# Own start distance for each slot of the two weight rings in a one-core attention and RG-LRU layer

## The reference

```
z = rms_norm(x) @ w_in                 # 2048 x 11328, split into q, kv, rope, gates, u, merge gates
y_mla = (softmax(q k^T, chunk mask) v * silu(gate)) @ w_o_mla      # 16 heads
y_lru = (scan of the RG-LRU over the 4-tap causal convolution of u * silu(gate)) @ w_o_lru
merged = sigmoid(m_mla) * y_mla + sigmoid(m_lru) * y_lru
x = x + merged @ w_out
x = x + (p @ w_ple) * sigmoid(rms_norm(x) @ w_ple_gate)
out = rms_norm(x)
```

## Time and profile before

| | us |
|---|---|
| median of three runs | 2129.43 (2128.58 to 2131.06) |
| span of the profiled execution | 2126.2 |
| TensorE matmul busy | 2070.6 (97%), 9070 matmuls |
| TensorE weight load busy | 1661.5 (78%) |
| GpSimd busy | 910.8 (43%) |
| ScalarE busy | 718.2 (34%) |
| VectorE busy | 665.4 (31%) |
| DMA | 247 MB, mean 116 GB/s |

### The profile page before, as it was taken

The page is one execution under the profiler, slowest core; times in us unless marked ns, Lnnn a source line. Parts: engine busy times, 40 slices in busy tenths (PEclk is TensorE's granted clock), DMA queues, the critical chain, the costliest instruction groups (busy, mean ns, idle before and its releaser), DMA issues.

```text
span 2126.2 us, 25597 instructions
## 1 busy us (share of the span) xinstructions
PE 2070.6 (97%) x9070; PEld 1661.5 (78%) x9070; DVE 665.4 (31%) x952; ACT 718.2 (34%) x1251; POOL 910.8 (43%) x683
## 2 busy tenths in 40 slices
PE   7999999999999999999998999999999999999997
PEld 5788888888887878778776777778888888888885
DVE  5100000000013728364676445591010151111344
ACT  6322223222223443524344444422222222233232
POOL 2444444444444544545361321144444444444442
PEclk9999999999999999999999999999999999999998
DMA  6533333333322323233352412343332343224222
GB/s 229 178 118 100 118 118 117 121 118 118 116 102 88 110 79 102 96 118 94 108 121 79 138 61 64 113 179 132 123 118 100 118 156 138 82 98 180 99 99 99
DMA packets 128684, 247.00 MB, mean 116 GB/s; under 512 B 15053, under 2 KB 40309, under 8 KB 120565
## 3 DMA queue, kind: packets, MB, share of 16 engines
q1 hardware_dynamic: 116688, 185.09, 26.6%
q10 hardware_dynamic: 11941, 61.17, 7.7%
HBM read 214.26 MB, written 29.36 MB: 115 GB/s over the span
## 4 chain that ended last, share of the span: by engine, by line
PE 51%; issue 27%; POOL 17%; DVE 3%; ACT 1%; POOLq 1%; ACTq 0%; DVEq 0%
PE ps L1214 49%; POOL wlo L351 17%; PE ps L1412 1%; DVE qrf L990 0%; DVE qrf L986 0%; POOLq L350 0%; DVE pjlo L1059 0%; PE ps L1474 0%; ACT pjhi L669 0%; DVE x L1203 0%; DVE stage L988 0%; ACTq L555 0%; POOLq L347 0%; DVE vlo L1026 0%; DVE latkv L974 0%
## 5 line engine op out<-in xcount | busy, mean ns | idle before, releaser
L351 POOL TENSOR_TENSOR wlo<-raw,whi 128x512 fp32r<-128x512 f32 x672 | 909.5, 1357 | 1189.5 <-ACT whi L367 1188.9
L367 ACT ACTIVATE whi<-raw 128x512 fp32r<-128x512 f32 x672 | 422.3, 632 | 1217.6 <-PE ps L1214 1165.9
L1214 PE MATMUL ps<-hhi,whi 128*128 128x512 f32 x1408 | 556.7, 395 | 2.9 <-POOL wlo L351 2.9
L1214 PE MATMUL ps<-hhi,wlo 128*128 128x512 f32 x1408 | 556.2, 395 | 0.0
L1214 PE MATMUL ps<-hlo,whi 128*128 128x512 f32 x1408 | 556.1, 395 | 0.0
L1214 PEld LDWEIGHTS ps<-hhi,whi 128*128 128x128 f32 x1408 | 263.9, 187 | 69.4 <-POOL wlo L351 5.1
L1214 PEld LDWEIGHTS ps<-hhi,wlo 128*128 128x128 f32 x1408 | 263.9, 187 | 64.7
L1214 PEld LDWEIGHTS ps<-hlo,whi 128*128 128x128 f32 x1408 | 263.9, 187 | 64.4
L875 DVE TENSOR_TENSOR stage<-ps,stage 128x512 f32<-128x512 f32 x16 | 11.0, 690 | 515.4 <-ACT stage L466 513.9
L1214 PE MATMUL ps<-lhi,whi 128*128 128x512 f32 x256 | 101.9, 398 | 2.5 <-DVE llo L795 2.5
L1214 PE MATMUL ps<-llo,whi 128*128 128x512 f32 x256 | 101.8, 398 | 0.0
(11 more groups left out here) (249 smaller groups left out, 2462.4 us busy)
## 6 DMA issues: line engine op xcount, KB each, us to landing
raw<-in_w_in SPq DMA_DIRECT2D x88, 1024.0 KB, 5.0
raw<-in_w_o_lru SPq DMA_DIRECT2D x16, 1024.0 KB, 5.0
raw<-in_w_o_mla SPq DMA_DIRECT2D x16, 1024.0 KB, 5.0
raw<-in_w_out SPq DMA_DIRECT2D x16, 1024.0 KB, 5.1
raw<-in_w_ple_gate SPq DMA_DIRECT2D x16, 1024.0 KB, 5.0
sig_scr<-stage ACTq DMA_DIRECT2D x8, 1024.0 KB, 7.0
raw<-in_w_kv_b SPq DMA_DIRECT2D x32, 256.0 KB, 4.2
stage<-sig_scr ACTq DMA_DIRECT2D x8, 1024.0 KB, 4.8
```

What stands on the lines that cost most here:

```text
L351: pool.tensor_tensor(wlo[:, k % RING], raw[:, k // RAWC, k % RAWC], whi[:, k % RING].bitcast(F32), ALU.subtract).then_inc(lo_ready, 1)
L367: act.activation(whi[:, c % RING], raw[:, c // RAWC % 2, c % RAWC], ACT.Copy).then_inc(hi_ready, 1)
L1214: return pe.matmul(o, l, r, start=start, stop=stop)
```

## The change

The two rings become views of one tensor `ring`. Slot n of `whi` begins at 2048 n bytes plus a pad of 0, 64, 128 or 256 bytes; slot n of `wlo` at 2048 (4 + n) bytes plus 528, 608, 704 or 896 bytes. Unused tensors (`line_pad`, `small_pad`, `l_pad`, `m_pad`, `x1_pad`) shift the other tiles. Nothing is computed in another way.

```
+        sb("line_pad", [P, 96])
         raw = sb("raw", [P, 2, RAWC, W])
-        whi = sb("whi", [P, RING, W], F32R)
-        wlo = sb("wlo", [P, RING, W], F32R)
+        ring = sb("ring", [P, 2 * RING * W + 352], F32R)
+        whi = [ring[:, n * W + pad:(n + 1) * W + pad] for n, pad in enumerate((0, 16, 32, 64))]
+        wlo = [ring[:, (RING + n) * W + pad:(RING + n + 1) * W + pad] for n, pad in enumerate((132, 152, 176, 224))]
...
+        sb("small_pad", [P, 24])
...
-        ohi, olo, lhi, llo, merged = lay(
+        ohi, olo, _, lhi, llo, _, merged = lay(
+            ("ohi", [P, KD, S], F32R), ("olo", [P, KD, S], F32R), ("l_pad", [P, 24], F32),
+            ("lhi", [P, KD, S], F32R), ("llo", [P, KD, S], F32R), ("m_pad", [P, 32], F32),
+            ("merged", [P, KD, S], F32))
-        x1, x1hi, mhi, mlo, x1lo = lay(
+        x1, _, x1hi, mhi, mlo, x1lo = lay(
+            ("x1", [P, TT, D], F32), ("x1_pad", [P, 56], F32), ("x1hi", [P, KD, S], F32R),
...
-                    h, l = whi[:, slot, m * P:(m + 1) * P], wlo[:, slot, m * P:(m + 1) * P]
+                    h, l = whi[slot][:, m * P:(m + 1) * P], wlo[slot][:, m * P:(m + 1) * P]
```

More of the change, by code:

```diff
@@ L183, in trunk_layer @@
             ("qrf", [P, HEADS // 2, S], F32), ("qr", [P, 4, S], F32R))
-        ohi, olo, lhi, llo, merged = lay(
-            ("ohi", [P, KD, S], F32R), ("olo", [P, KD, S], F32R),
-            ("lhi", [P, KD, S], F32R), ("llo", [P, KD, S], F32R), ("merged", [P, KD, S], F32))
-        x1, x1hi, mhi, mlo, x1lo = lay(
-            ("x1", [P, TT, D], F32), ("x1hi", [P, KD, S], F32R),
+        ohi, olo, _, lhi, llo, _, merged = lay(
[4 more added lines that the diff above has]
+            ("x1", [P, TT, D], F32), ("x1_pad", [P, 56], F32), ("x1hi", [P, KD, S], F32R),
             ("mhi", [P, KD, S], F32R), ("mlo", [P, KD, S], F32R), ("x1lo", [P, KD, S], F32R))
-        _, plep, gfin = lay(("ple_r1", [P, R1], F32), ("plep", [P, NG, TT, W], F32), ("gfin", [P, D], F32))
+        _, plep, gfin = lay(("ple_r1", [P, R1 + 64], F32), ("plep", [P, NG, TT, W], F32), ("gfin", [P, D], F32))
         ps = ctx.enter_context(nc.psum_tensor("ps", [P, 8, 512], F32))
@@ L350, in _ @@
                     pool.wait_ge(hi_ready, i * (2 * RAWC) + (k + 1))
-                    pool.tensor_tensor(wlo[:, k % RING], raw[:, k // RAWC, k % RAWC],
-                                       whi[:, k % RING].bitcast(F32), ALU.subtract).then_inc(lo_ready, 1)
+                    pool.tensor_tensor(wlo[k % RING], raw[:, k // RAWC, k % RAWC],
+                                       whi[k % RING].bitcast(F32), ALU.subtract).then_inc(lo_ready, 1)
         @block.scalar
@@ L366, in split @@
                     act.wait_ge(chunk_used, i * stride + (c - RING + 1))
-                act.activation(whi[:, c % RING], raw[:, c // RAWC % 2, c % RAWC], ACT.Copy).then_inc(hi_ready, 1)
+                act.activation(whi[c % RING], raw[:, c // RAWC % 2, c % RAWC], ACT.Copy).then_inc(hi_ready, 1)
             act.dma_start(vrow[0:N1, 0, :], vectors).then_inc(vec_landed, 16)
@@ L1230, in tokens @@
                     h, l = ahi[:, m * P:(m + 1) * P], alo[:, m * P:(m + 1) * P]
-                    mm(o, h, whi[:, slot], first, False)
-                    mm(o, h, wlo[:, slot], False, False)
-                    ins = mm(o, l, whi[:, slot], False, last)
+                    mm(o, h, whi[slot], first, False)
+                    mm(o, h, wlo[slot], False, False)
+                    ins = mm(o, l, whi[slot], False, last)
                 return ins
@@ L1495, in _ @@
                     h, l = x1hi[:, k, t * P:(t + 1) * P], x1lo[:, k, t * P:(t + 1) * P]
-                    mm(ps[:, t], h, whi[:, slot], False, False)
-                    mm(ps[:, t], h, wlo[:, slot], False, False)
-                    ins = mm(ps[:, t], l, whi[:, slot], False, k == KD - 1)
+                    mm(ps[:, t], h, whi[slot], False, False)
+                    mm(ps[:, t], h, wlo[slot], False, False)
+                    ins = mm(ps[:, t], l, whi[slot], False, k == KD - 1)
                 ins.then_inc(last_done, 1)
```

## The result

| | before | after |
|---|---|---|
| median, us | 2130.24 (2128.58 to 2132.03) | 2117.07 (2114.45 to 2117.96) |
| span of the profiled execution, us | 2126.2 | 2112.7 |

Ratio 0.9937, 95% interval 0.9923 to 0.9951: so 13 us less, a change of 0.6% that is clear of the noise. The forecast was 2103 us, a gain of 26 us. The direction was right, the size forecast was twice what was measured.

What follows compares the result with a forecast made beforehand. The prediction took TensorE's matmul rate as the bound. Its terms, -27 + 1 + 0 = -26 us on 2126.2, gave a span of 2100 us and, with 3.2 us for the median, 2103 us; range 2042 to 2159 us.

Steps and rivals of the forecast that it cites:

- What bounds the kernel, and the unit price: TensorE's matmul rate sets the end; 8064 ring matmuls lie in sequence, so 1 ns on each is 8.06 us.
- The distance matters, against the rule of two ports that never wait: Operand start distance changes matmul gaps, 233.3 against 227.1 ns; by the documented rule it cannot matter and the sum is 0.
- Step (a): The 8064 ring matmuls: mean gap falls from 233.3 to 230 ns under the new distances, -27 us.
- Its bounds: Limits for the ring matmuls: -161 us if all reach 213.3 ns, +134 us if every one takes 250 ns.
- Step (b): Where TensorE waits for other engines, a faster TensorE waits longer; in attention half the gain may be lost, 1 us.
- Step (c): GpSimd, ScalarE, VectorE and DMA at other starts: GpSimd's 1.28 us piece stays covered below 2.76 us; taken as 0.
- Step (d): Products without rings (krw2, gates, attention's scores and values) keep their distances: no change.
- Rival, far distances: Ring matmuls at 96 to 256 bytes could be mostly free of extra cycles: 220 ns, -107 us, 2022 us; chance 0.16.
- Rival, mixing costs: Mixed distances at slot and chunk changes are slower than one common distance: 236.0 ns mean, +22 us, 2151 us; chance 0.28.

Runs made afterwards that it cites:

- experiment 2: All-at-0 kernel with activation tiles moved so the common distance is the old 32 bytes at other places, krw2 also 32 from hhi: 2132.04 us, one run.
- experiment 8: Changed kernel with other pads, two probes, one run each: small distances, 2113.01 us; high slots at 0 with low slots at -32 to -192, 2122.35 us.
- experiments 5 and 6: Changed kernel with slot 0's pads for all slots, 2110.92 us; then one common distance of 16, 128 or 64 bytes: 2106.86, 2124.99, 2121.52 us.
- experiment 1: Changed kernel with all ring slots and activation tiles starting at 0 modulo 512 bytes, activation pads taken out: 2081.13 us, ratio 0.9777 to the kernel before.
- experiment 5: Changed kernel with slot 0's pads for all slots: high at 0, low at 16 bytes, activation tiles at 0; 2110.92 us, ratio 0.9924 to before.

## Why the direction of the prediction was right and its size wrong

- *What bounds the kernel, and the unit price.* Right: TensorE's gaps alone, 8.06 us for each ns. After the change -1.8 ns gave -14.4 by this and -13.5 in the span; with all at 0, -52 and -46. One reading was too broad: the clock was below its upper level not only at the edges, but for a short while in attention too (0.99 in the earlier trace rows).
- *The distance matters, against the rule of two ports that never wait.* Right, and now shown by the krw2 product alone (experiment 2). By the Trainium skill, page SBUF — State Buffer, section "Who interferes with whom", TensorE reads its two operands through independent ports and never waits on anyone. The trace does not agree with the plain reading of it, that the rate is the same at any distance: 227.1 against 233.5 ns. Whether the difference is a wait at a read port, no run shows.
- *Step (a), "I take 230 ns".* The direction was right and this is the term that was mis-sized: 231.5 ns, -14 us instead of -27. The value was taken between krw2's settled 227.1 and unsettled 231 ns, as if all eight distances were near 0. The runs show that only a slot whose two distances are near 0 modulo 256 comes to 226.7 and that the others stay between 231.0 and 234.0 ns. In the changed kernel that is one slot of four, in the features form, outside of the lhi half of C_Y. One slot at 80 ns less, two at 20 less and one at none make 120 / 48 = 2.5 ns a gap in the stages with `hhi`, and 1 ns in the later ones.
- *Its bounds.* -161 and +134 us were far too wide. No common distance came out slower than 32 in a measurable way, and none under 226.7 ns; the slowest single slot took 235.7 ns a gap (experiment 8). The 250 ns of the upper bound is one of eight handovers in the trace before: from the full starts it is 243 ns, and five of the eight take 234 and 227 ns.
- *Step (b), what is given back.* 1 us forecast. For this change the sum (-14.4) and the span (-13.5) bear it out. With all at 0 it was 6, more than forecast in proportion: over 2 in the LRU stage, where TensorE waited for GpSimd, and nearly 4 in attention. Most of the latter goes with the lower granted clock (in experiment 2, without faster chunks, the stage is 2.5 us longer than before at that same lower clock), and that is not the path that step (b) names.
- *Step (c).* Right: GpSimd's mean is 1355 ns against 1357 in the earlier trace rows, at starts of 16 and 96 bytes.
- *Step (d).* Right: krw2 kept its 227 ns.
- *Rival, far distances.* Wrong in its ground: 96 to 224 bytes all run near 233 ns.
- *Rival, mixing costs.* Not in sign, but it names a part of what limits the gain: behind a slot off the good distance, a slot at 0 loses its settled pattern for some gaps (0 takes 2741 ns behind -48, and 2720 behind itself). Its ground does not hold: the eight handovers from `gates` to the ring take 232.5 ns on average after the change (234.0 before), not 240.

What stays open: why 0 modulo 256 is the good one, by what a product in between switches the pattern at 0/-16, at -16 and at +64 (where it does is shown in experiments 5 and 6), why +64 in the tokens form has a third pace, and what the 13 ns are that even 226.7 lies above the 213.3 that half of the earlier trace rows gives.

## What to carry to other kernels

When matmuls stand back to back, measure start to start and compare it with every other product of the same width in the same trace: one that runs faster shows what is to be had. Here 48 us (2.2%) lay in where the stationary and the moving tile start: put both at the same place modulo 256 bytes, for all slots of a ring and all activation tiles alike, and use pads only for that. A distance close to 0 is no substitute: at -16 bytes the fast pace was lost at the first product of another distance and did not come back by itself in the LRU stage. Giving each slot a distance of its own makes most of them miss it; it is a way to probe, and even as a probe it misleads, since a slot's time depends on its neighbours.

## What the runs showed of the hardware

- Two fp32r operands of 512 and 128 columns: 226.7 ns a matmul at distance 0 or 256, 233.3 ns at 32, either sign, at the upper clock level; 426.7 ns at the lower level at distance 32, which is 512 cycles of 1.2 GHz with nothing added, and the same 426.7 ns there with all distances at 0 (experiment 1). So this distance costs nothing at the lower level.
- The gap is not a function of the current pair alone. krw2 at distance 0 starts at 231 ns and comes to 226.7 after nine matmuls (after two to nine in the other kernels). The same distances ran at 226.7 in one stretch and at 232.2 in another of the same stage, and the change came where another product ran in between (experiment 5).
- In attention the granted clock differs from one profiled kernel to another (0.97 to 0.99 in the traces shown), whatever the distance: 0.99 before and 0.97 with all at 0, but 0.97 also with the old distance at other places, where the stage took 291.5 us instead of 289.0.
